# Scores of two dilated heads side by side in two halves of the rows, and a column load moved behind the exponentials of lambda

## The chip, the cores and the metric

The kernel runs on one NeuronCore of a Trainium2 chip. The metric is the device time of one execution in microseconds (us). The engines named here are TensorE (PE in the rows, its weight loads PEld), VectorE (DVE), ScalarE (ACT), GpSimd (POOL) and SyncE (SP), which issues most of the DMAs.

## The reference, cut to what matters

A decoder block on 256 tokens of width 1024: a norm, one projection, attention by 16 heads of 64 columns, an output projection, a norm, and a mixture of 32 experts (top 4). Eight heads are differential (two softmax maps of 32 columns each, subtracted with the scalar lambda, then a norm per head with a weight of 64 numbers, `diff_subln_w`), eight are dilated (one map of 64 columns, a mixture of three patterns of distances):

```python
lam = exp(sum(lq1 * lk1)) - exp(sum(lq2 * lk2)) + lam_init
o_diff = rms_norm(diff_attention(dq, dk, dv, diff_slopes, lam), diff_subln_w) * (1.0 - lam_init)
o_dil = dilated_attention(lq, lk, lv, dil_slopes)
x = x + concatenate([o_diff, o_dil]) @ w_out
x = x + moe_ffn(rms_norm(x, ffn_norm_w), ...)      # 32 experts, 12 MB of f32 weights each
return rms_norm(x, final_norm_w)
```

## The kernel before, in words

Everything is f32 and written out by hand: each engine has a program of its own, in the order in which it is written, and engines wait on counting semaphores.

SP issues all large loads in one queue: x, `w_in` in 13 pieces, the expert biases, then, as the ring slots come free, `w_out` and the expert weights. The ring `gu_ring` has 16 slots of 1 MB, loaded two at a time; `dn_ring` has four. The first experts' loads are written behind waits on counts of TensorE's progress. In the expert loop (`load_gu_half`, line 295 and those after it) each load waits for `gu_used` or `dn_used`, which TensorE raises as it uses a slot up.

TensorE first transposes x, projects (`project`, L567 for the transposed chunks, L572 for the values), and then goes through the 16 heads in a loop over g (line 680). Step g holds, in this order: the three transposes of head g-1's probabilities (`turn_probs`, L545), the scores of head g+1 (`score`, L617 and L618), pieces of other products to fill the time (`FILL`: the rest of the projection, up to g = 8; `OUT`: the output projection, L664, from g = 9), sometimes a transpose of the mixed heads (`turn_mix`, L545 too), and the product of head g-1's probabilities with the values (`pv`, L642 to L644). A head's scores have 256 columns for the second half of the queries and 128 for the first, in one PSUM bank per map. A differential head has two maps, in two groups of 32 rows and in banks 4 and 5. A dilated head has one map in 64 rows, rows 0 to 63 for an even head and 64 to 127 for an odd one, and always in bank 4. Heads 0 to 7 are differential, 8 to 15 dilated.

VectorE's step g is: `negated_scores(g+1)` (L975 takes the scores out of PSUM, L981 finds the extremes), then head g's probabilities (`diff_probs` L988 to L993, `dil_probs` L1006 to L1009); beside that, in some steps, casts of the biases (L945, L950), the scaling of projected chunks (L938), or the norm of two differential heads (`norm_pair`, L1016 to L1023). Probabilities of head g from g = 10 on also wait for head g-2's output copy. ScalarE's step g copies the transposed probabilities of head g-1 (L437), computes the exponentials of head g+1 (L429), copies the transposed mix (L456) and head g-1's output (L442, L447).

The head norm's weight is loaded as a column, twice, into two halves of the partitions of `prm` (two DMAs of 64 elements, L390, third and fourth in ScalarE's queue). VectorE multiplies the column by 1 - lam_init (L967) after it has made lambda's sums and before the loop over heads. ScalarE first uses it in `keep_mixT(0)`, in its step 4. Lambda's exponentials are L410.

After the heads the output projection, the router and the choice of the experts follow, then the loop over 16 pairs of experts: L777 gathers tokens, L822 is gate and up, L837 is down, L796 adds an expert's output to the sums, with four products of 64 rows each, alternately rows 0 to 63 and 64 to 127.

Of the kernel before, what the change touches and what calls it, by code (L numbers as in the profile page):

```python
# [28 lines left out]
P = 128  # L29
T, D = 256, 1024  # L30
TT = T // P
KT = D // P
HD = 64
NH = 8
DK = HD // 2
EPS = 1e-5
LAM_INIT = 0.8 - 0.6
# [12 lines left out]
def moe_block(nc, x, attn_norm_w, w_in, lq1, lk1, lq2, lk2, subln_w, w_out, ffn_norm_w, router_w, router_b,  # L50
              w_gate_up, b_gate_up, w_down, b_down, final_norm_w, out):
    ctx = ExitStack()
    with ctx:
        def sb(name, shape, dt=F32):
            return ctx.enter_context(nc.sbuf_tensor(name, shape, dt))

        def sem(name):
            return ctx.enter_context(nc.semaphore(name))
# [11 lines left out]
        prm = sb("prm", [P, 17])  # L70
# [6 lines left out]
        qkT = gu_ring[:, 13:15, :].rearrange("p s (m t) -> p (s m) t", t=T)  # L77
# [52 lines left out]
        psum = ctx.enter_context(nc.psum_tensor("psum", [P, 8, 512], F32))  # L130
        bank = [psum[:, i, :] for i in range(8)]
# [40 lines left out]
        qk_ready = sem("qk_ready")  # L172
# [3 lines left out]
        scores_done = sem("scores_done")  # L176
        scores_read = sem("scores_read")
# [11 lines left out]
        sub_in = sem("sub_in")  # L189
        sub_ready = sem("sub_ready")  # L190
# [195 lines left out]
        def _(act):  # L386
            act.dma_start(prm_rows[0:8, :], attn_norm_w.rearrange("o (k p) -> (o k) p", p=P)).then_inc(prm_in, 16)
            act.dma_start(prm_rows[8:16, :], ffn_norm_w.rearrange("o (k p) -> (o k) p", p=P)).then_inc(prm_in, 16)
            for i in range(2):
                act.dma_start(prm[HD * i:HD * (i + 1), 16:17], subln_w.rearrange("o d -> d o")).then_inc(sub_in, 16)  # L390

            def squares(a):

# [14 lines left out]
                                         scale=prm[:, k:k + 1]).then_inc(hT_ready_a, 1)  # L408
            act.wait_ge(lam_sum, 1)
            nc.scalar.activation(st[:, 6:8], st[:, 4:6], ACT.Exp).then_inc(lam_exp, 1)  # L410

            def keep_v(done, n, b0, c0):
                act.wait_ge(done, n)
                act.wait_ge(rs_ready, 1)
                for a in range(TT):
                    last = nc.scalar.activation(vS[:, a, c0:c0 + 512], bank[b0 + a][:, :], ACT.Copy,
                                                scale=st[:, 2 + a:3 + a])
                last.then_inc(v_ready, 1)
# [114 lines left out]
            for a in range(TT):  # L533
                act.wait_ge(acc_done, a + 1)
                b = (0, 5)[a]
# [5 lines left out]
        def _(pe):  # L541
            mm = nc.tensor.matmul
# [60 lines left out]
                project(DQK, k)  # L603

            def score(g):
                if g in (0, 4, NH):
                    pe.wait_ge(qk_ready, {0: 2, 4: 4, NH: 8}[g])
                if g >= 1:
                    pe.wait_ge(scores_read, g)
                h = g % NH  # L610
                maps = 2 if g < NH else 1
                rows = HD // maps
                for m in range(maps):
                    r0 = HD * (h % 2) + rows * m
                    tq, tk = (h // 2, 4 + h // 2) if g < NH else (8 + h // 2, 12 + h // 2)
                    q, k = qkT[r0:r0 + rows, tq, :], qkT[r0:r0 + rows, tk, :]
                    mm(bank[4 + m][:, 0:T], q[:, P:T], k, start=True, stop=True)  # L617
                    last = mm(bank[4 + m][:, T:T + P], q[:, 0:P], k[:, 0:P], start=True, stop=True)  # L618
                last.then_inc(scores_done, 1)

            def turn_probs(g):
                pe.wait_ge(probs_ready, g + 1)
                if g == 0:
                    pe.wait_ge(v_ready, 1)
                if g >= 1:
                    pe.wait_ge(probsT_ready, g)
                for b in range(3):
                    last = turn(bank[6][:, P * b:P * (b + 1)], probs[g % 2][:, P * b:P * (b + 1)])
                last.then_inc(probsT_done, 1)
# [16 lines left out]
            def turn_mix(kt, g):  # L646
                if kt < NH // 2:
                    pe.wait_ge(mix_ready, kt + 1)
                pe.wait_ge(pv_read, g - 1)
                if kt >= 1:  # L650
                    pe.wait_ge(mixT_ready, kt)
                for a in range(TT):
                    last = turn(bank[7][:, P + P * a:2 * P + P * a], hmix[:, a, P * kt:P * (kt + 1)])
                last.then_inc(mixT_done, 1)
# [16 lines left out]
            def out_project(kt, a):  # L671
                for c in range(2):
                    out_half(kt, a, c)
# [6 lines left out]
            for g in range(2 * NH):  # L680
                if g == 1:
                    pe.wait_ge(qk_ready, 3)
                    project(EQ, 0)
                    project(EQ, 1)
                if g >= 1:
                    turn_probs(g - 1)
                if g + 1 < 2 * NH:
                    score(g + 1)
                for i, (chunk, k) in enumerate(FILL.get(g, ())):
                    if k == 0:  # L690
                        pe.wait_ge(qk_ready, {EK: 4, EV: 6}[chunk])
                    project(chunk, k)
                    if i == 0 and g in TURN_AT:
                        turn_mix(TURN_AT[g], g)
                if g in TURN_AT and TURN_AT[g] >= NH // 2:
                    turn_mix(TURN_AT[g], g)
                for i, (kt, a) in enumerate(OUT.get(g, ())):
                    out_project(kt, a)
                    if i == 0 and g in TURN_AT and TURN_AT[g] < NH // 2:
                        turn_mix(TURN_AT[g], g)  # L700
                if g >= 1:
                    pv(g - 1)
# [187 lines left out]
        def _(dve):  # L890
            V = nc.vector
# [50 lines left out]
            def rest_of_bias(n):  # L942

                rows = slice(NE * (2 - n), 2 * NE)
                link(V.tensor_tensor(bias_rest[rows, :], (bias_rows if n == 2 else bias_rest)[rows, :], bias3[rows, :],  # L945
                                     ALU.subtract))

            def bias_part(n):
                rows = slice(NE * (2 - n), 2 * NE)
                return V.tensor_copy(bias3[rows, :], bias_rest[rows, :])  # L950
# [7 lines left out]
            for i in range(2):  # L958
                ins = V.tensor_tensor_reduce(out=lam_rows[:, 2 * i, :], in0=lam_rows[:, 2 * i, :],
                                             in1=lam_rows[:, 2 * i + 1, :], scale=1.0, scalar=0.0,  # L960
                                             op0=ALU.mult, op1=ALU.add, accum_out=st[:, 4 + i:5 + i])
# [1 line left out]
                    link(ins)  # L963
            ins.then_inc(lam_sum, 1)

            dve.wait_ge(sub_in, 16 * 2)
            V.tensor_scalar(prm[:, 16:17], prm[:, 16:17], 1.0 - LAM_INIT, None, ALU.mult).then_inc(sub_ready, 1)  # L967
            def negated_scores(g):

                dve.wait_ge(scores_done, g + 1)  # L970
                slope = SLOPES[2 * (g % NH) + (g >= NH)]
                dist = dist_diff if g < NH else dist_dil
                maps = 2 if g < NH else 1
                s = scores[g % 2]
                V.scalar_tensor_tensor(out=s[:, 0:maps, :], in0=dist.unsqueeze(1).broadcast_to([P, maps, T + P]),  # L975
                                       scalar=slope, in1=psum[:, 4:4 + maps, 0:T + P], op0=ALU.mult,
                                       op1=ALU.subtract).then_inc(scores_read, 1)
                dve.wait_ge(scores_read, g + 1)
                for c, w, i in ((0, T, 2), (T, P, 0)):
                    lo = 24 + 4 * (g % 2) + i  # L980
                    ins = V.tensor_reduce(st[:, lo:lo + maps], s[:, 0:maps, c:c + w], AX.X, ALU.min)  # L981
                ins.then_inc(max_ready, 1)
# [53 lines left out]
            for g in range(2 * NH):  # L1036
                if g + 1 < 2 * NH:
                    negated_scores(g + 1)
                if g < NH:
                    diff_probs(g)  # L1040
                else:
                    dil_probs(g)
                if g == 1:
                    rest_of_bias(1)
                if g == 2:
                    bias_part(1).then_inc(bias_split, 1)
                if g == NH - 2:
                    dve.wait_ge(ek_done, 1)
                    for h in range(2):
                        keep_qk(12 + 2 * h, 2 + h, 1.0)  # L1050
                if g >= 3 and g % 2 == 1 and g <= NH + 1:
                    norm_pair((g - 3) // 2)
                if g == 4:
                    dve.wait_ge(eq_used, 4)
                    for h in range(2):
                        keep_qk(8 + 2 * h, h, HD ** -0.5)
# [118 lines left out]
            for r in range(2, ROUNDS):  # L1175
                link(V.scalar_tensor_tensor(out=st[:, 55:56], in0=st[:, 54:55], scalar=float(CAP * r), in1=st[:, 55:56],
                                            op0=ALU.is_gt, op1=ALU.add))
# [53 lines left out]
            for a in range(TT):  # L1231
# [3 lines left out]
                for c in range(2):  # L1235
                    V.scalar_tensor_tensor(out=hmix[:, a, 512 * c:512 * (c + 1)], in0=bank[(0, 5)[a] + c][:, :],
                                           scalar=st[:, 2 + a:3 + a], in1=gu_ring[:, 0, 512 * c:512 * (c + 1)],
                                           op0=ALU.mult, op1=ALU.mult).then_inc(h_ready, 1)
# [21 lines left out]
```

## Time and profile before

| | |
|---|---|
| median of 3 runs (lowest, highest) | 1086.72 us (1086.65, 1087.52) |
| the profiled execution: time, span | 1088.17 us, 1086.4 us |
| mean granted TensorE clock | 0.987 |
| busy in the span: TensorE, VectorE, ScalarE, GpSimd | 1029.8, 228.8, 119.5, 10.1 us |
| moved by DMA | 423.69 MB, mean 390 GB/s |
| issue to landing, medians: `w_in` pieces of 1 MB, of 0.5 MB; x | 18.4, 8.1; 3.7 us |

The rows of the next section come from that one execution. Times run from the first instruction. A matmul of f32 data shows as two records, and the records overlap in time; the distance from one start to the next tells more than a duration. In the chain of waits, which is followed back from the last instruction, a piece's length is what it adds to the chain.

### The profile page before, as it was taken

The page shows a single profiled execution, that of the slowest core. Times are in us where ns is not written, and L with a number is a line of the kernel's source. Part 1 is how long each engine was busy: PE and PEld are TensorE (multiplying, and loading weights), DVE is VectorE, ACT ScalarE, POOL GpSimd, SP SyncE. Part 2 cuts the span into 40 slices and gives each one's busy share as a digit, 9 for nine tenths or more (in the row PEclk, how much of TensorE's full clock was granted, in tenths as well). Part 3 has the DMA queues.
Part 4 walks back from the last instruction along what each step waited for, and adds up shares of the span by engine and source line. Part 5 has one row for each costly group of instructions (what it writes and reads, how often), then busy time and mean ns, then how long its engine had stood idle before and what let it go on. Part 6 is the DMA issues. An engine that isn't in the chain of part 4 may idle for free.

```text
span 1086.4 us, 12314 instructions
## 1 busy us (share of the span) xinstructions
PE 1029.8 (95%) x4971; PEld 442.3 (41%) x4971; DVE 228.8 (21%) x508; ACT 119.5 (11%) x287; POOL 10.1 (1%) x25
## 2 busy tenths in 40 slices
PE   7999999999999999989999999899999999999996
PEld 6686554333343432424242424343243434343422
DVE  3566444111111110111111111111111111111111
ACT  1133430000000000000000000000000000000001
POOL 0000000000000000000000000000000000000000
PEclk9999999999999998999999999999999999999999
DMA  9926546999999999999999999999999999999995
GB/s 283 415 103 243 208 171 264 426 429 427 430 428 428 428 428 430 428 429 428 427 431 427 429 428 428 430 427 428 429 427 431 427 428 430 427 431 427 428 428 207
DMA packets 35808, 423.69 MB, mean 390 GB/s; under 512 B 6016, under 2 KB 6032, under 8 KB 11120
## 3 DMA queue, kind: packets, MB, share of 16 engines
q1 hardware_dynamic: 34032, 423.33, 92.7%
q10 hardware_dynamic: 1760, 0.14, 0.1%
q8 instruction: 10, 0.16, 0.1%
q14 instruction: 6, 0.05, 0.0%
HBM read 422.41 MB, written 1.05 MB: 390 GB/s over the span
## 4 chain that ended last, share of the span: by engine, by line
PE 62%; DMA 31%; DVE 4%; ACT 1%; issue 1%; SPq 0%; DVEq 0%; POOLq 0%; POOL 0%; ACTq 0%
PE psum L822 24%; DMA dn_ring<-in_w_down_dram 23%; PE psum L837 17%; DMA gu_ring<-in_w_gate_up_dram 7%; PE psum L567 5%; PE psum L777 5%; PE psum L545 3%; PE psum L664 3%; PE psum L572 2%; DVE shared L1206 1%; DVE shared L1202 1%; DVE shared L1204 1%; PE psum L617 1%; DMA gu_ring<-in_w_in_dram 1%; ACT shared L519 0%
## 5 line engine op out<-in xcount | busy, mean ns | idle before, releaser
L822 PE MATMUL psum<-gu_ring,shared 128*64 128x512 f32 x2048 | 446.8, 593 | 4.7 <-DMA gu_ring<-in_w_gate_up_dram 4.7
L837 PE MATMUL psum<-dn_ring,shared 128*64 128x512 f32 x1024 | 240.1, 620 | 31.7 <-DMA dn_ring<-in_w_down_dram 30.0
L822 PEld LDWEIGHTS psum<-gu_ring,shared 128*64 128x64 f32 x2048 | 143.5, 137 | 287.4 <-issue 275.1
L837 PEld LDWEIGHTS psum<-dn_ring,shared 128*64 128x64 f32 x1024 | 72.9, 142 | 180.4 <-issue 132.2
L1202 DVE TENSOR_SCALAR shared<-psum 128x512 f32<-128x512 f32 x32 | 22.1, 692 | 398.0 <-PE psum L822 398.0
L1151 DVE TENSOR_TENSOR shared<-posm,iota 128x256 f32<-128x256 f32 x47 | 20.0, 425 | 291.1 <-PE psum L545 290.6
L517 ACT ACTIVATE shared<-psum 128x512 f32<-128x512 f32 x32 | 19.1, 597 | 436.7 <-PE psum L822 436.7
L796 PE MATMUL psum<-shared 64*128 64x512 f32 x264 | 65.6, 615 | 0.7 <-ACT shared L510 0.7
L777 PE MATMUL psum<-shared,xres 128*128 128x128 f32 x512 | 63.0, 282 | 1.0 <-DVE shared L1121 1.0
L777 PEld LDWEIGHTS psum<-shared,xres 128*128 128x128 f32 x512 | 61.7, 197 | 1.5 <-DVE shared L1121 1.5
L567 PE MATMUL psum<-gu_ring 128*128 128x256 f32 x256 | 59.3, 390 | 2.1 <-DMA gu_ring<-in_w_in_dram 2.1
L510 ACT ACTIVATE shared<-psum 128x512 f32<-128x512 f32 x32 | 19.1, 597 | 317.5 <-PE psum L837 317.5
L567 PEld LDWEIGHTS psum<-gu_ring 128*128 128x128 f32 x256 | 49.3, 195 | 10.1 <-issue 2.9
L545 PE MATMUL psum<-ident,shared 128*128 128x128 f32 (+1 forms) x243 | 46.8, 300 | 3.0 <-ACT shared L519 0.7
L545 PEld LDWEIGHTS psum<-ident,shared 128*128 128x128 f32 (+1 forms) x243 | 30.6, 180 | 38.7 <-issue 25.7
L796 PEld LDWEIGHTS psum<-shared 64*128 64x128 f32 x264 | 22.8, 186 | 43.0 <-issue 41.4
L1164 DVE TENSOR_TENSOR shared<-psum,ffn_p 128x512 f32<-128x512 f32 x32 | 22.1, 692 | 59.9 <-PE psum L777 59.9
L801 PE MATMUL psum<-shared 96*64 96x512 bf16 x192 | 32.9, 395 | 0.0
L664 PE MATMUL psum<-dn_ring,shared 128*128 128x512 f32 x64 | 30.1, 602 | 0.0
L572 PE MATMUL psum<-gu_ring 128*128 128x512 f32 x64 | 29.3, 601 | 0.0
L519 ACT ACTIVATE shared<-psum 128x512 f32<-128x512 f32 x32 | 19.1, 597 | 80.2 <-PE psum L545 80.2
L429 ACT ACTIVATE shared<-shared,st 128x256 f32<-128x256 f32 (+1 forms) x48 | 20.6, 445 | 40.1 <-DVE st L981 40.1
(142 smaller groups left out, 354.0 us busy)
## 6 DMA issues: line engine op xcount, KB each, us to landing
gu_ring<-in_w_gate_up_dram SPq DMA_DIRECT2D x128, 2048.0 KB, 26.4
dn_ring<-in_w_down_dram SPq DMA_DIRECT2D x64, 2048.0 KB, 23.4
gu_ring<-in_w_in_dram SPq DMA_DIRECT2D x11, 1024.0 KB, 18.4
dn_ring<-in_w_out_dram SPq DMA_DIRECT2D x4, 1024.0 KB, 8.9
xres<-in_x_dram SPq DMA_DIRECT2D x2, 512.0 KB, 3.7
gu_ring<-in_w_in_dram SPq DMA_DIRECT2D x2, 512.0 KB, 8.1
out_dram<-hmix SPq DMA_DIRECT2D x4, 256.0 KB, 2.0
dn_ring<-in_b_gate_up_dram SPq DMA_DIRECT2D x3, 256.0 KB, 15.1
```

Source lines behind the costliest of these rows:

```text
L429: last = nc.scalar.activation(s[:, m, c:c + w], s[:, m, c:c + w], ACT.Exp, bias=st[:, lo + i + m:lo + i + m + 1], scale=-1.0, **acc)
L545: return nc.tensor.transpose(dst, src, ident[0:rows, 0:rows])
L567: last = mm(bank[b][:, c:c + T], w[:, P * (m0 + m):P * (m0 + m + 1)], hT[:, k, :], start=(k == 0 and m % 2 == 0), stop=(k == KT - 1), skip ...
L572: last = mm(bank[b0 + a][:, :], hT[:, k, P * a:P * (a + 1)], w[:, v0:v0 + 512], start=(k == 0), stop=(k == KT - 1))
L664: last = mm(bank[2 * a + c][:, :], mixT[:, kt, P * a:P * (a + 1)], dn_ring[:, kt // 2, w0:w0 + 512], start=(kt == 0), stop=(kt == KT - 1))
L777: last = mm(bank[b][:, c:c + P], rows, sel[:, a, :, :].rearrange("p e n -> p (e n)"), start=(a == 0), stop=(a == TT - 1))
L796: last = mm(bank[(0, 5)[a] + c][:, :], combT[rows, P * a:P * (a + 1)], yrow[rows, :], start=False, stop=True, skip_group_check=True)
L801: return mm(bank[b][CAP * c:CAP * (c + 1), :], bias_sel[half][0:3 * NE, :], bias3[0:3 * NE, col:col + 512], start=True, stop=False, skip_g ...
L822: last = mm(bank[2 + b][CAP * c:CAP * (c + 1), :], xg[:, k, CAP * half:CAP * (half + 1)], gu_ring[:, 8 * half + k, w0:w0 + 512], start=Fal ...
L837: last = mm(bank[4][CAP * c:CAP * (c + 1), :], actT[:, a0:a0 + CAP], dn_ring[:, k // 2, w0:w0 + 512], start=False, stop=(k == KT - 1), ski ...
L1164: V.tensor_tensor(xg[:, 4 * b:4 * b + 4, :], bank[XG_BANKS[first][b]][:, :].rearrange("p (k n) -> p k n", k=4), ffn_p[:, 4 * b:4 * b + 4]. ...
L1202: chain(V.tensor_scalar(up_t, bank[3][:, :], 1.0 - LIMIT, 1.0 + LIMIT, ALU.max, ALU.min))
```

## The change

The first edit takes the dilated heads out of `score` and adds `score_pair`, which is called in steps 7, 9, 11 and 13 and computes the scores of two dilated heads: the even one from rows 0 to 63 into bank 4, the odd one from rows 64 to 127 into bank 5, the products alternating between them. Each head raises `scores_done` by one as before. The even steps from 8 to 14 compute no scores. VectorE reads bank 4 or 5 by the head. The second edit moves the two column loads in ScalarE's queue behind the exponentials of lambda, and VectorE's wait for them with the multiplication into its step 2, behind the last cast of the biases.

```diff
 # ScalarE
             act.dma_start(prm_rows[8:16, :], ffn_norm_w.rearrange("o (k p) -> (o k) p", p=P)).then_inc(prm_in, 16)
-            for i in range(2):
-                act.dma_start(prm[HD * i:HD * (i + 1), 16:17], subln_w.rearrange("o d -> d o")).then_inc(sub_in, 16)
...
             nc.scalar.activation(st[:, 6:8], st[:, 4:6], ACT.Exp).then_inc(lam_exp, 1)
+            for i in range(2):
+                act.dma_start(prm[HD * i:HD * (i + 1), 16:17], subln_w.rearrange("o d -> d o")).then_inc(sub_in, 16)
 # TensorE
             def score(g):
-                if g in (0, 4, NH):
-                    pe.wait_ge(qk_ready, {0: 2, 4: 4, NH: 8}[g])
+                if g in (0, 4):
+                    pe.wait_ge(qk_ready, {0: 2, 4: 4}[g])
                 if g >= 1:
                     pe.wait_ge(scores_read, g)
                 h = g % NH
-                maps = 2 if g < NH else 1
-                rows = HD // maps
-                for m in range(maps):
-                    r0 = HD * (h % 2) + rows * m
-                    tq, tk = (h // 2, 4 + h // 2) if g < NH else (8 + h // 2, 12 + h // 2)
-                    q, k = qkT[r0:r0 + rows, tq, :], qkT[r0:r0 + rows, tk, :]
+                for m in range(2):
+                    r0 = HD * (h % 2) + DK * m
+                    q, k = qkT[r0:r0 + DK, h // 2, :], qkT[r0:r0 + DK, 4 + h // 2, :]
                     mm(bank[4 + m][:, 0:T], q[:, P:T], k, start=True, stop=True)
                     last = mm(bank[4 + m][:, T:T + P], q[:, 0:P], k[:, 0:P], start=True, stop=True)
                 last.then_inc(scores_done, 1)
+
+            def score_pair(g):
+
+                if g == NH:
+                    pe.wait_ge(qk_ready, 8)
+                pe.wait_ge(scores_read, g)
+                heads = [(qkT[HD * m:HD * (m + 1), 4 + g // 2, :], qkT[HD * m:HD * (m + 1), 8 + g // 2, :]) for m in range(2)]
+                for m, (q, k) in enumerate(heads):
+                    mm(bank[4 + m][:, 0:T], q[:, P:T], k, start=True, stop=True)
+                for m, (q, k) in enumerate(heads):
+                    mm(bank[4 + m][:, T:T + P], q[:, 0:P], k[:, 0:P], start=True, stop=True).then_inc(scores_done, 1)
...
                     turn_probs(g - 1)
-                if g + 1 < 2 * NH:
+                if g + 1 < NH:
                     score(g + 1)
+                elif g % 2 and g + 1 < 2 * NH:
+                    score_pair(g + 1)
 # VectorE
-            dve.wait_ge(sub_in, 16 * 2)
-            V.tensor_scalar(prm[:, 16:17], prm[:, 16:17], 1.0 - LAM_INIT, None, ALU.mult).then_inc(sub_ready, 1)
             def negated_scores(g):
...
-                maps = 2 if g < NH else 1
+                maps, b = (2, 4) if g < NH else (1, 4 + g % 2)
                 s = scores[g % 2]
                 V.scalar_tensor_tensor(out=s[:, 0:maps, :], in0=dist.unsqueeze(1).broadcast_to([P, maps, T + P]),
-                                       scalar=slope, in1=psum[:, 4:4 + maps, 0:T + P], op0=ALU.mult,
+                                       scalar=slope, in1=psum[:, b:b + maps, 0:T + P], op0=ALU.mult,
                                        op1=ALU.subtract).then_inc(scores_read, 1)
...
                 if g == 2:
                     bias_part(1).then_inc(bias_split, 1)
+                    dve.wait_ge(sub_in, 16 * 2)
+                    V.tensor_scalar(prm[:, 16:17], prm[:, 16:17], 1.0 - LAM_INIT, None, ALU.mult).then_inc(sub_ready, 1)
```

## Rows read from the trace of the kernel before

**Rows 1.** The page, part 2: DMA share and rate in 40 slices.

```profile
DMA  9926546999999999999999999999999999999995
GB/s 283 415 103 243 208 171 264 426 429 427 430 428 428 428 428 430 428 429 428 427 431 427 429 428 428 430 427 428 429 427 431 427 428 430 427 431 427 428 428 207
```

**Rows 2.** Windows: stretch, busy time and records of each engine, clock, DMA share, GB/s.

```profile
118.00:124.00 6.00, 5.45 (x23) 3.07 (x21) 3.32 (x13) 2.41 (x7) 1.01 (x1) 1.00 1.01 426
170.00:176.00 6.00, 6.00 (x35) 3.05 (x36) 2.87 (x9) 1.49 (x2) 0.00 (x0) 1.00 0.00 0
```

**Rows 3.** Timeline of SP from 170 us: start, length, DMA issues.

```profile
175.62 10.54 SPq L263 DMA_DIRECT2D gu_ring<-in_w_gate_up_dram  x4
```

**Rows 4.** Chain that ended last, in order of time: start, length, what.

```profile
18.83 13.82 PE psum L567 x64
...
79.45 0.64 PE psum L617 x4
80.09 0.22 PE psum L618 x4
...
100.54 0.63 PE psum L617 x2
101.17 0.22 PE psum L618 x2
...
123.49 0.48 ACT shared L456
...
171.76 13.88 PE psum L822 x64
```

**Rows 5.** Timeline of TensorE at heads 12 and 13: start, length, operation, shapes.

```profile
125.22 0.70 PE L617 MATMUL psum<-gu_ring 64*128 64x256 f32 x2
...
128.68 0.50 PE L545 MATMUL psum<-ident,shared 128*128 128x128 f32 x3
...
132.39 0.49 PE L545 MATMUL psum<-ident,shared 128*128 128x128 f32 x3
```

**Rows 6.** The same chain: products of 512 columns, on 128 and on 64 rows.

```profile
40.00 3.43 PE psum L572 x8
...
187.56 1.92 PE psum L796 x8
```

**Rows 7.** Timeline of VectorE, 115 to 130 us.

```profile
120.11 0.43 DVE L1023 TENSOR_TENSOR hmix<-hmix,st 128x256 f32<-128x256 f32 x1 [1.12 <-POOL st L365]
121.36 0.56 DVE L975 SCALAR_TENSOR_TENSOR shared<-shared,psum 128x384 f32<-128x384 f32 x1 [0.83 <-PE psum L618]
...
126.18 0.55 DVE L975 SCALAR_TENSOR_TENSOR shared<-shared,psum 128x384 f32<-128x384 f32 x1 [2.74 <-PE psum L618]
...
128.09 0.17 DVE L1009 RECIPROCAL st<-st 128x2 f32<-128x2 f32 x1
```

**Rows 8.** Timeline of ScalarE at the first and the 12th head's exponentials.

```profile
46.38 0.51 ACT L429 ACTIVATE shared<-shared,st 128x256 f32<-128x256 f32 x1 [12.03 <-DVE st L981]
...
122.60 0.80 ACT L429 ACTIVATE shared<-shared,st 128x256 f32<-128x256 f32 x2 [1.52 <-DVE st L981]
```

**Rows 9.** Instructions on prm: min/median/max ns, first and last start; its loads' landing.

```profile
L407 ACT ACTIVATE gu_ring<-psum,prm x4: 466/470/474, 7.4 to 19.0; 128x256 f32<-128x256 f32 x4
...
L390 ACTq DMA_DIRECT2D prm<-in_diff_subln_w_dram x2: 526/567/608, 1.8 to 2.3; - x2
...
DMA to landing us min/median/max: 7.0/7.2/7.4
```

**Rows 10.** Timeline of VectorE, 73 to 77 us.

```profile
73.45 0.95 DVE L975 SCALAR_TENSOR_TENSOR shared<-shared,psum 128x768 f32<-128x768 f32 x1
...
76.94 0.35 DVE L993 SCALAR_TENSOR_TENSOR shared<-shared,st 128x128 f32<-128x128 f32 x1
```

**Rows 11.** TensorE's first projection in the timeline, and a window before it.

```profile
9.43 8.96 PE L567 MATMUL psum<-gu_ring 128*128 128x256 f32 x32 [2.08 <-DMA gu_ring<-in_w_in_dram]
6.00:7.00 1.00, 1.00 (x6) 0.89 (x5) 0.93 (x3) 0.00 (x0) 0.00 (x0) 1.00 0.49 131
```

## The prediction

> **What bounds the kernel now.** I read the page first for stages. Its slices [rows 1] show two: up to about slice 6 (some 170 us) the DMA share moves between 0.2 and 0.9; from slice 7 on the DMA share stands at 9 and the rate at 426 to 431 GB/s to the end. A window says it closer for the last of the first stage [rows 2]: no byte moves from 170 to 176 us, and then the stream is full. So the expert loop is paced by the weight stream, and what counts is when the stream starts. It starts at 175.62 us, where SP issues the load into the first ring slot that TensorE has used up [rows 3]; TensorE's first use of that slot begins at 171.76 us [rows 4]. Nothing else that the stream needs is late then, since the queues had been empty for some six us. So a microsecond that TensorE saves before 171.76 us moves the stream, and with it the end, by that microsecond; a microsecond saved on TensorE in the loop is worth nothing.
>
> Then the chain of waits through the stretch that the change touches, 100 to 172 us [rows 4]. It is TensorE nearly throughout: the two score rows of a head (0.63 and 0.22 us), then the next products with no gap. The other engines take it over in three places between 99 and 141 us only. The largest waits are for the transposed mix that ScalarE copies, the second of these at 123.49 us [rows 4]; the other kind is for a head's output before the next transpose of the mix.
>
> **The change part by part.**
>
> *Removed: the scores of heads 9, 11, 13 and 15 as steps of their own.* A dilated head's scores hold the chain for 0.63 + 0.22 = 0.85 us [rows 4] (at 100.54 and 101.17). Two records are one f32 product. A product of 512 columns takes 3.43 / 4 = 0.86 us [rows 6], so 384 columns take 0.64 us; the other 0.21 us of the 0.85 are spent around it, where TensorE goes from 128 rows to 64 and back. All eight dilated heads repeat the pattern. Four of the eight go: 4 x 0.85 = 3.40 us.
>
> *Added: two more products in each of the four pairs that stay.* What a pair costs, the trace of before shows twice. A differential head has two maps in two groups of 32 rows and two banks, 768 columns in four products. They hold the chain for 0.64 + 0.22 = 0.86 us [rows 4] (at 79.45 and 80.09), what a dilated head's two products take; one after another they would take 1.28 + 0.21 = 1.49 us. And for halves of 64 rows: the combine of the experts puts four products of 512 columns alternately on the two halves, 8 records in 1.92 us, against 3.43 us for the same columns on all 128 rows [rows 6]; 1.92 - 0.21 = 1.71 is two products, not four. So halves do run beside each other at 64 rows too. I take 0.85 us for a pair, as for one head now, thus nothing added. The bounds: 0.85 and 1.49 us, so 0 to 4 x 0.64 = 2.56 us added in all. The pair also signals twice where a head signals once; no row here isolates the second signal. By the Trainium skill, page "TensorE: Matmul & The Clock Gate", section "The cost: per-tile semaphore tail", increments serialize at some 26 ns each; by that, an estimate, the four pairs would lose 0.1 us, and the sum would be 3.3 and not 3.4.
>
> *New order: does something else become late?* In the loop over heads, an even step now has no scores, an odd one has those of the next two heads. In an odd step VectorE works on the first of the pair as now: scores start at 125.22, VectorE starts at 126.18, ends head 11's probabilities at 128.09 + 0.17 = 128.26, TensorE wants them at 128.68 [rows 5, 7]: 0.42 us to spare, unchanged as long as the pair's first head is as fast as a single one. In an even step TensorE arrives 0.85 us sooner: for head 12's at 132.39 - 0.85 = 131.54 us. VectorE had waited for TensorE there, but need not now, since head 13's scores lie ready: it goes on at 128.26 and needs another 126.18 to 128.26 = 2.08 us, so 130.34: over one us to spare. ScalarE is tightest at head 11: its scores have to wait for the head norm, which ends on VectorE at 120.11 + 0.43 = 120.54; ScalarE starts the exponentials 1.24 us after VectorE starts on the scores (121.36 to 122.60) and takes 0.80, so until 122.6, just when the transposed mix, 0.85 us earlier than 123.49, wants its copy [rows 4, 7, 8]. Say 0 to 0.1 us lost there. The three waits above stay: each follows a transpose or an output, not scores. For new waits I take 0.1 us, and as the bound what would undo all four even steps' savings but one, 2.5 us.
>
> *Moved: the two column loads of the norm weight.* At the head of ScalarE's queue they took 0.53 and 0.61 us to issue and landed after 7.0 and 7.4 us [rows 9]. In the new place, behind the exponentials of lambda (which end 12.03 us before 46.38, at 34.35), ScalarE has nothing until 46.38 [rows 8]: the 1.2 us of issue are hidden. VectorE now wants them where it starts head 4's scores, at 73.45 us [rows 10]. Issued by 35.5 us they may take 38 us to land; the loads of 1 MB that queue through the same full stretch take 18.4 at the median (the table above). So the wait costs nothing. The multiplication of one column (0.17 us at most, what its row on two columns takes, at 128.09 in [rows 7]) now stands in its queue in front of head 4's scores. Behind it, head 3's probabilities are ready at 76.94 + 0.35 = 77.29 and wanted by the transposes that precede 79.45, 0.50 us long as those at 128.68, thus at 78.95 [rows 4, 5, 10]. So the 0.17 us are hidden 1.66 us deep.
>
> What goes from the start is the load pair itself. TensorE's first projection waits 2.08 us for its weights and starts at 9.43 us; the DMA share falls to 0.49 in the microsecond from 6 to 7 [rows 11], and the columns, issued at 1.8 and 2.3 us, land at about 9.3, just after. If the columns cause it, up to 9.43 - 7.87 = 1.56 us is to be had: at 7.4 + 0.47 = 7.87 us the first transposed tile is there, the next thing that the projection waits for [rows 9] (the row of L407). If they don't, nothing. Their own bytes are 0.5 KB. Later in this kernel a larger set of small pieces (the router's weight and the second norm weight, issued by ScalarE behind head 7) is in flight while the rate is 426 GB/s, from 118 to 124 us [rows 2], so I take zero. By the Trainium skill, page "DMA: Bandwidth & Descriptors", section "Rules for kernel authors", a load whose last dimension is not contiguous becomes one descriptor per element, 128 here, whereas its section "Issuing engines are not separate DMA queues" has such loads merely interleave with the others; the first speaks for the 1.56 us, the second for zero.
>
> *Sum:* 3.40 - 0 - 0.1 = 3.3 us. The profiled execution took 1088.17 us, 1.8 around its span of 1086.4; it would take 1084.9. It stands 1.45 above the median of the runs; the saving is the same there: 1086.7 - 3.3 = 1083.4 us.
>
> **Rivals.**
> 1. *The start moves too.* The dip around 6 us goes with the columns: 3.3 + 1.5 = 4.8, thus 1081.9 us. For it: the columns land just as the first weights do, and the dip has no other owner that I can name. Against: 0.5 KB, and the row from 118 us on. The first 32 records of the projection take 8.96 us [rows 11], 280 ns each, against 216 ns later (13.82 us for 64 [rows 4]); an earlier start could shorten that too, by up to 2.0 us, and add to it.
> 2. *New waits eat it.* Heads in twos make TensorE wait for VectorE or ScalarE in the even steps; half is lost: 1.6 us gained, 1085.1 us. For it: 0.42 us to spare is little. Against: the sums above.
> 3. *The halves do not overlap.* Pairs of 1.49 us: 3.40 - 2.56 = 0.84 gained, 1085.9 us; only the four changes of row shape are saved. Against: both patterns of [rows 4, 6].
> 4. *Slower: the columns come late.* VectorE's queue stands at 73.45 us until both have landed, before head 4's scores. TensorE has 1.66 us to spare (77.29 to 78.95), the gain buys 3.3 more; so from a landing at 78.4 us on, 43 us after the issue, the kernel is slower, and at 50 us after it by 7 us: 1094. Against: 18.4 us for 1 MB in that stretch, and 7.4 for the columns before.
>
> **How the numbers follow.** Chances: the forecast 0.62, start moves too 0.16, waits eat it 0.11, no overlap 0.06, late columns 0.03, something unnamed of either sign 0.02. The likeliest gives 1083.4. The range, 1081.3 to 1085.2, takes in the first rival with half a us beyond it and most of the second; beyond lie the third, the fourth and the tails. No change from 0.2% (2.17 us, about what a measurement of this kernel tells from no change) leaves: faster 0.62 + 0.16 + 0.01 = 0.79, same 0.11 + 0.06 = 0.17, slower 0.03 + 0.01 = 0.04.
>
> **What would show it.** In the profile after: pairs of 0.85 us at four places, the last of them near 133, and none in even steps; the three waits of TensorE still there and no fourth; the first expert product at 168.4 and SP's issue at 172.2 instead of 171.76 and 175.62, with the stream full from there; first projection still at 9.4 us. A pair row of 1.3 us or more says rival 3, a wait for VectorE at a transpose of probabilities in an even step rival 2, a first projection before 9 us rival 1. If TensorE's gain up to 171.76 us is there but the end has not moved with it, my reading of the stream is wrong.

## The result and the profile after

The changed kernel takes 1082.45 us at the median of five runs (1080.44 to 1083.12), the kernel before, on the same chip, 1087.52 (1086.65 to 1089.01). The ratio is 0.9949 with a 95% interval of 0.9938 to 0.9960, a gain of 5.1 us (4.3 to 6.7) where 3.3 were forecast and 1083.4 us as the time. The profiled execution was the fastest of the five: 1080.44 us with a span of 1078.7, 7.7 us under the span of before. That this one is a special case came out only in the experiments. (One run of e9 below, at 1117.5 us with a lower granted clock, is left out of its median and range.)

The page of the changed kernel, part 2, DMA share and rate in 40 slices. It answers to [rows 1]: the stream fills from slice 7 on as before, at the same rate.

```profile
DMA  9935467999999999999999999999999999999995
GB/s 326 383 140 241 171 234 299 426 427 428 430 429 429 428 428 428 429 428 428 428 428 428 430 429 428 428 428 428 430 428 428 428 428 428 428 430 430 427 427 211
```

SP's timeline (it answers to [rows 3]) and the chain of waits (to [rows 4, 6]) of the changed kernel. In its lines L614 and L615 are the differential scores, L625 and L627 the pairs, L650 to L652 the products with the values, L832 is gate and up.

```profile
168.21 10.54 SPq L263 DMA_DIRECT2D gu_ring<-in_w_gate_up_dram  x4
```

```profile
7.92 7.17 PE psum L567 x32
...
36.70 3.43 PE psum L572 x8
...
97.25 0.63 PE psum L625 x4
97.88 0.22 PE psum L627 x4
98.11 5.35 PE psum L572 x12
...
104.07 0.34 PE psum L545 x3
104.40 1.72 PE psum L572 x4
...
118.15 0.46 ACT shared L456
...
164.35 13.88 PE psum L832 x64
```

Three things are to be seen. A pair (768 columns) holds the chain for 0.63 + 0.22 us, as one head's 384 columns did. An even step has no scores: the transposes at 104.07 are followed by the next product at once. And that product's four records take 1.72 us. In the chain of before the same step read:

```profile
107.35 0.34 PE psum L545 x3
107.68 0.63 PE psum L617 x2
108.31 0.22 PE psum L618 x2
108.53 1.91 PE psum L572 x4
```

So 0.63 + 0.22 + 0.19 = 1.04 us went with the step, not 0.85: its scores, and what the four records behind them had taken more, 1.91 - 1.72. From the first value product (40.00 before, 36.70 now) to the first expert product (171.76, 164.35) it is 131.76 us before and 127.65 now: 4.11 us. The remaining 3.30 us of this profile lie ahead of 36.70. SP's first issue of the loop moved by 175.62 - 168.21 = 7.41 us, the span by 7.7: what is gained ahead of the stream arrives at the end.

### The profile page after: what moved, and what is told of

The parts are those of the page before. It is cut to its first block, busy times and chain, and to the rows that moved or that the text cites. A ratio compares the mean times of both kernels' runs of the same rounds, so it can differ in the third digit from the quotient of the medians.

```text
span 1078.7 us, 12314 instructions
## 1 busy us (share of the span) xinstructions
PE 1025.4 (95%) x4971; PEld 438.7 (41%) x4971; DVE 228.5 (21%) x508; ACT 119.2 (11%) x287; POOL 10.1 (1%) x25
## 4 chain that ended last, share of the span: by engine, by line
PE 64%; DMA 28%; DVE 5%; ACT 1%; issue 1%; SPq 0%; POOL 0%; DVEq 0%; POOLq 0%; ACTq 0%
PE psum L832 25%; DMA dn_ring<-in_w_down_dram 21%; PE psum L847 18%; DMA gu_ring<-in_w_gate_up_dram 7%; PE psum L787 6%; PE psum L567 5%; PE psum L545 3%; PE psum L572 2%; PE psum L672 2%; DVE shared L1216 1%; DVE shared L1212 1%; DVE shared L1214 1%; PE psum L614 0%; ACT shared L519 0%; PE psum L652 0%
## 5 line engine op out<-in xcount | busy, mean ns | idle before, releaser
L832 PE MATMUL psum<-gu_ring,shared 128*64 128x512 f32 x2048 | 446.8, 593 | 4.8 <-DMA gu_ring<-in_w_gate_up_dram 4.8
L832 PEld LDWEIGHTS psum<-gu_ring,shared 128*64 128x64 f32 x2048 | 143.5, 137 | 287.5 <-issue 274.7
L572 PE MATMUL psum<-gu_ring 128*128 128x512 f32 x64 | 29.2, 599 | 0.0
## 6 DMA issues: line engine op xcount, KB each, us to landing
dn_ring<-in_b_gate_up_dram SPq DMA_DIRECT2D x3, 256.0 KB, 14.1
```

The source lines that it names most:

```text
L572: last = mm(bank[b0 + a][:, :], hT[:, k, P * a:P * (a + 1)], w[:, v0:v0 + 512], start=(k == 0), stop=(k == KT - 1))
L832: last = mm(bank[2 + b][CAP * c:CAP * (c + 1), :], xg[:, k, CAP * half:CAP * (half + 1)], gu_ring[:, 8 * half + k, w0:w0 + 512], start=Fal ...
```

## The experiments

Two questions: how the 7.4 us divide, and why the runs as a whole gained only five. Theory: each half of the change adds its part, 3.3 us for the columns and 4.1 for the pairs. Rival: the early start of the one profile is chance.

**e1, the columns alone**, scores one head at a time:

```diff
             act.dma_start(prm_rows[8:16, :], ffn_norm_w...)
-            for i in range(2):
-                act.dma_start(prm[HD * i:HD * (i + 1), 16:17], subln_w.rearrange("o d -> d o")).then_inc(sub_in, 16)
...
             nc.scalar.activation(st[:, 6:8], st[:, 4:6], ACT.Exp).then_inc(lam_exp, 1)
+            for i in range(2):
+                act.dma_start(prm[HD * i:HD * (i + 1), 16:17], subln_w.rearrange("o d -> d o")).then_inc(sub_in, 16)
```

(and VectorE's wait and multiplication as in the change)

> Only the column loads are moved, the scores stay one head at a time. Theory (each half of the change adds its own part: the two column loads at the head of ScalarE's queue delay TensorE's first projection weights by 1.5 us and its faster pace by another 1.8): first projection at 7.9 us, in the step loop everything 3.3 us earlier than before, first expert product at 171.8 - 3.3 = 168.5 us, span 1083, time 3.3 us under before. Rival (the early start of the one profiled execution is chance, and the columns have no part in it): first projection anywhere from 7.9 to 9.4 us whatever stands in the queue, time within 1 us of before.

**e2, the pairs alone**, columns at the head of the queue as before (the second edit undone):

```diff
             act.dma_start(prm_rows[8:16, :], ffn_norm_w...)
+            for i in range(2):
+                act.dma_start(prm[HD * i:HD * (i + 1), 16:17], subln_w.rearrange("o d -> d o")).then_inc(sub_in, 16)
...
```

(gone behind the exponentials of lambda, and VectorE's wait and multiplication back in their old place)

> Only the scores are paired, the column loads stay at the head of ScalarE's queue. Theory: each even step from 8 to 14 is 1.04 us shorter (0.85 for the scores and 0.19 for the next product, which follows a change of row shape), so 4.1 us in all, first projection at 9.4 us, first expert product at 171.8 - 4.1 = 167.6 us, time 4.1 us under before. Rival (start is chance): the same steps, but the first projection may stand at 7.9 us, and the time is that of the full change.

**e3, the changed kernel once more**, no edit:

> The changed kernel once more, for a second profile and for times on the same chip as the two halves. Theory: first projection at 7.9 us again, first expert product at 164.3, time 3.3 + 4.1 = 7.4 us under before in an execution whose loop is undisturbed; the two halves add up. Rival (start is chance): first projection at some other time in this profile, and the time equals that of the pairs alone, 4.1 to 5 us under before.

**e4, rows in the place of the columns:**

```diff
             act.dma_start(prm_rows[8:16, :], ffn_norm_w...)
+            for i in range(2):
+                act.dma_start(scratch[i:i + 1, :], subln_w).then_inc(scratch_in, 16)
...
```

(`scratch` is a new tile that nothing reads, and the program waits at its end until both loads have landed)

> The changed kernel with two more loads in the place where the column loads stood, third and fourth in ScalarE's queue: the same 64 numbers, but as a contiguous row of 256 bytes into one partition each (a scratch that nothing reads). Theory A (the shape of the column loads, 64 pieces of 4 bytes each, holds up the weights): no delay, first projection at 7.9 us, time as the changed kernel. Theory B (any two further loads on ScalarE's queue in that moment do it): first projection at 9.4 us, time 3.3 us above the changed kernel.

All four ran on one chip beside the kernel before (1087.27 us, 17 runs, 1085.01 to 1089.15):

| kernel | median us (range) | ratio to before (95%) | first projection | its first 32 records | first value product | from there to the first expert product |
|---|---|---|---|---|---|---|
| before (first profile) | 1087.27 (1085.01 to 1089.15) | | 9.43 | 8.96 | 40.00 | 131.76 |
| e1 columns alone | 1086.89 (1084.68 to 1087.97) | 0.9995 (0.9986 to 1.0003) | 8.27 | 10.04 | 39.92 | 131.77 |
| e2 pairs alone | 1082.68 (1081.43 to 1083.66) | 0.9954 (0.9941 to 0.9968) | 8.29 | 9.26 | 39.16 | 127.63 |
| e3 both | 1083.00 (1081.77 to 1083.65) | 0.9956 (0.9944 to 0.9969) | 7.93 | 9.81 | 39.34 | 127.63 |
| e4 both, rows at the head | 1082.63 (1082.12 to 1083.03) | 0.9955 (0.9943 to 0.9967) | 7.92 | 9.49 | 39.02 | 127.63 |

The pairs are all of the gain that can be measured: 4.1 us from value product to expert product in each profile with them, and 4.6 us in the times of e2, to which moving the columns adds nothing that shows (e3 is 0.3 us above e2, both intervals nearly alike). My theory of two parts failed on the columns: e1 gained 0.4 us, and its interval reaches from a loss of 0.3 to a gain of 1.5, so 3.3 us are excluded and half a microsecond is not. The rival, chance, is right for the 3.3 us of the first profile. But it is not right on the DMAs. The windows from 6 to 8 us (columns as in [rows 2]), first of e2 with columns at the head:

```profile
6.00:7.00 1.00, 1.00 (x5) 0.65 (x4) 0.93 (x3) 0.00 (x0) 0.00 (x0) 1.00 0.63 172
7.00:8.00 1.00, 0.64 (x4) 0.24 (x2) 0.58 (x3) 0.60 (x2) 0.00 (x0) 1.00 0.67 193
```

then of e3 without them:

```profile
6.00:7.00 1.00, 1.00 (x6) 0.75 (x5) 0.93 (x3) 0.00 (x0) 0.00 (x0) 1.00 1.03 414
7.00:8.00 1.00, 0.61 (x4) 0.21 (x2) 0.68 (x3) 0.60 (x2) 0.00 (x0) 1.00 1.03 410
```

and of e4 with rows in their place:

```profile
6.00:7.00 1.00, 1.00 (x6) 0.72 (x5) 0.93 (x3) 0.00 (x0) 0.00 (x0) 1.00 1.00 406
7.00:8.00 1.00, 0.65 (x4) 0.25 (x2) 0.65 (x3) 0.61 (x2) 0.00 (x0) 1.00 1.06 406
```

So the dip of [rows 11] is the columns' doing, by their shape (64 pieces of 4 bytes, each to a partition of its own) and not by the number of loads or their bytes: 512 bytes cost the stream over half of its rate for some us. The dip is there in both profiles with the columns at the head and in none without. The packets of ScalarE's queue in the first 12 us tell the shapes apart, here before, in the changed kernel and in e4:

```profile
q10 hardware_dynamic: 192, 0.01, 0.9%
...
q10 hardware_dynamic: 32, 0.01, 0.3%
...
q10 hardware_dynamic: 36, 0.01, 0.3%
```

With the two columns the queue has 160 packets more, with the two rows four. Whether the number of pieces or that of the partitions they go to does the harm, e4 does not separate.

Where did the earlier start go? Into the pace of the first projection. In e1 it starts 0.35 us later than in the first profile of the changed kernel (7.92 and 7.17, above) and takes 2.87 us longer:

```profile
8.27 10.04 PE psum L567 x32
```

The starts of the single records show why: they follow each other at first after 427 ns and later after 216, at half pace and then at full pace, the two levels of TensorE's clock (1.2 and 2.4 GHz). The distance changes at 13.12 us before, at 14.14 in e1, 12.58 in e2, 13.29 in e3, 12.65 in e4 (12.20 and 13.42 in e7 and e8 below), but at 7.85 us, ahead of the projection, in the changed kernel's first profile. The windows' clock column stands at 1.00 all through and does not show it: each trace's record of the clock begins only at the time just named, with the full clock, and has nothing for the stretch ahead of it. While the pace is half, a microsecond of earlier start is worth half a microsecond of work. In e1 the start is 1.16 us earlier than before, worth 0.58, and the full pace comes 1.02 us later, which costs 0.51: the first value product stands 0.08 us earlier, at 39.92. This made the next theory: what ends the slow pace is TensorE's work, not the time since the start, and it can be had early.

**e5, idle products** in the two empty stretches of the start:

```diff
+            def idle_products(n):
+                for _ in range(n):
+                    mm(bank[3][:, 0:P], ident[:, :], ident[:, :], start=True, stop=True)
+
+            idle_products(7)
             pe.wait_ge(x_in[0], 16)
...
             for k in range(4):
                 turn_x(1, k)
+            idle_products(3)
             for k in range(KT):
```

> The changed kernel with products of the identity with itself, whose results nothing reads, in TensorE's two empty stretches of the start: seven before x has landed, three before the first projection. Theory (after the column move TensorE starts its projection up to 1.5 us earlier, but its records keep the slow pace of 430 ns until 13 or 14 us whenever it starts, and so give the start back; what ends the slow pace is how long TensorE has been at work without a gap): records at 216 ns from before 9 us, first 32 records of the projection in 7.0 to 7.5 us as in the one lucky profile, first expert product at 164.3 to 164.8 us, time 2 to 3 us under the changed kernel. Rival (the end of the slow pace is set by something outside TensorE, such as the time since the start): slow until 13 us as before, time unchanged or up to 0.5 us longer for the added products.

**e6, the same with the columns at the head**, as in e2:

> As the warmed kernel, but with the column loads at the head of ScalarE's queue, where they stood before the change. Theory (the columns' own price is the late first weights, 0.4 to 1.5 us, and it is hidden in the plain kernel only because the slow pace ends at the same time anyway): now the late start counts in full, first projection at 8.3 to 9.4 us, time 0.4 to 1.5 us over the warmed kernel with moved columns. Rival (the columns never cost anything): first projection and time equal to the warmed kernel's within 0.3 us.

**e9, idle products in the kernel before**, nothing else:

> The kernel before with the idle products in TensorE's two empty stretches of the start, and nothing else. Theory (the pairs save 4.13 us whatever the start does; the spread of the kernel before, 1085 to 1089 us, comes from where the slow pace ends): values sum within 1 us, first 32 records of the projection in 7.0 to 7.3 us, first expert product at 37.3 + 131.8 = 169.1 us, time 4.1 us over the warmed kernel with pairs and the columns at the head (1081.0), thus 1085.1. Rival (the idle products help the paired kernel only, or something in the loop spreads the times): spread as without them, time 1087.

| kernel | median us (range) | first projection | its first 32 records | first value product | to the first expert product |
|---|---|---|---|---|---|
| e5 changed, idle products | 1080.54 (1080.20 to 1080.68) | 8.36 | 7.07 | 37.04 | 127.64 |
| e6 the same, columns at the head | 1081.03 (1080.47 to 1082.15) | 8.55 | 7.14 | 37.30 | 127.64 |
| e9 before, idle products | 1085.1 (1084.54 to 1086.23) | 9.35 | 7.14 | 38.10 | 131.77 |

The timeline of TensorE in e5: the first row are the idle products, the transposes at 4.74 still run at the slow pace, the projection does not.

```profile
1.59 3.36 PE L583 MATMUL psum<-ident 128*128 128x128 f32 x14 [1.59 <-POOL ident L349]
4.74 1.91 PE L545 MATMUL psum<-ident,xres 128*128 128x128 f32 x8
...
7.69 0.83 PE L583 MATMUL psum<-ident 128*128 128x128 f32 x6
8.36 7.07 PE L567 MATMUL psum<-gu_ring 128*128 128x256 f32 x32
```

The theory holds: in the five kernels with idle products the full pace comes at 5.45 to 7.67 us, always ahead of the projection. e5 is 2.5 us under e3 (1083.00 to 1080.54, two chips' medians of before being 0.4 apart, in the other direction), and the times of its six runs lie within 0.5 us where e3's spread over 1.9 and the kernel before's, on e5's chip, over 4.2. e9 gains 2.8 us on the kernel before of its chip (1087.94), so the idle products do not help the paired kernel only, and its time is the expected one. Its values spread over 1.7 us, not within the 1 us expected; before they spread over 3.4 there. So about half of that kernel's spread goes with the slow pace. e9 also gives the pairs once more, on a quieter ground: 1085.1 - 1081.03 = 4.1 us between e9 and e6 (two chips, their medians of before 0.3 apart), and 4.13 in the profiles.

And e6 gives the columns a price. The wait for the first weights is back (0.62 us idle, projection 0.2 to 1.0 us later in e6 and e9 than in e5), the median is 0.5 us higher than e5's, though both intervals against before overlap, and the range is 1.7 and not 0.5:

```profile
8.55 7.14 PE L567 MATMUL psum<-gu_ring 128*128 128x256 f32 x32 [0.62 <-DMA gu_ring<-in_w_in_dram]
```

All profiles together bear it out: the projection starts at 8.29 to 9.43 us in the five with the columns at the head and at 7.92 to 8.36 in the eight without. And of the kernels with idle products those with the columns at the head spread over 1.7 us (e6, e9), those without over 0.4 to 0.5 (e5 and, below, e10 and e11). The profile of e9:

```profile
9.35 7.14 PE L567 MATMUL psum<-gu_ring 128*128 128x256 f32 x32 [1.80 <-DMA gu_ring<-in_w_in_dram]
```

**e8, the price of the change of row shape.** The kernel before with the dilated scores over all 128 rows:

```diff
                 for m in range(maps):
...
+                    if g >= NH:
+                        r0, rows = 0, P
                     q, k = qkT[r0:r0 + rows, tq, :], qkT[r0:r0 + rows, tk, :]
```

> The kernel before, but each dilated head's scores taken over all 128 rows instead of its own 64, so that two heads' scores are summed (the output is not the reference's): the same columns and banks, no change of row shape. Theory (1.04 us per score step are 0.64 for 384 columns and 0.40 for the change to 64 rows and back, half of it showing in the product that follows): a score step takes 0.64 us up to the next product and four following records 1.72 and not 1.91 us; eight heads are 3.2 us shorter. Rival (64-row products are slower in themselves): the same 0.2 us around the scores stays, only 0 to 0.2 us saved per head.

Measured once: 1085.01 us. Its chain:

```profile
106.84 0.33 PE psum L545 x3
107.18 0.43 PE psum L619 x2
107.61 0.22 PE psum L620 x2
107.83 1.72 PE psum L572 x4
```

0.65 us for the scores and 1.72 for the next four records, 0.39 less than with 64 rows; where a transpose of the mix follows the scores it is 0.3 to 0.35. From the first value product (39.88) to the first expert product (168.77) it is 128.89, 2.87 less than before where 3.2 were expected. Hence 1.04 = 0.65 + 0.39. The rival, that 64-row products are slower in themselves, e8 alone does not exclude, since it takes away the narrow products together with the change. The starts of the single records do. Before, at this place, the four score records start at 107.61, 107.93, 108.15 and 108.26, in e8 at 107.01, 107.23, 107.45 and 107.56: the second distance and the third are the same, and only the first is 0.10 us longer, as is the one from the transpose to the scores (0.20 and not 0.11). Behind the scores it is the same again, 0.20 and 0.53 us into the product of 128 rows and not 0.11 and 0.43. So the 0.39 us go with the change, and 64-row products that follow each other are not slower.

**e7, filling work dealt out anew**, against the two waits for the transposed mix that the change left alone:

```diff
-                6: [(EV, 0), (EV, 1)], 7: [(EV, 2), (EV, 3), (EV, 4)], ...
+                6: [(EV, 0), (EV, 1), (EV, 2)], 7: [(EV, 3), (EV, 4)], ...
-        OUT = {9: [(0, 1), (0, 0)], 10: [(1, 0)], ...
+        OUT = {9: [(0, 1)], 10: [(0, 0), (1, 0)], ...
```

> The changed kernel with the filling work dealt out differently: one more projection piece in step 6 and one fewer in step 7, and the product of the first output chunk with the second token tile's queries moved from step 9 to step 10, behind the transposed mix. Theory (the two waits of 0.61 and 0.66 us for ScalarE's copy of the transposed mix are uncovered because nothing stands between the transpose and the product that waits): both waits gone, first expert product 1.2 us earlier relative to the start of the heads, time 1.2 us less. Rival (the waits come back as waits for probabilities in steps 7 and 10, which now come sooner): less than 0.4 us gained.

1081.51 us (1079.52 to 1081.89), 1.5 under e3's median on another chip; in the profile 126.70 us from value to expert product, 0.95 less where 1.2 were expected. The first wait is gone, of the second 0.24 us remain:

```profile
119.97 0.41 PE L650 MATMUL psum<-gu_ring,shared 128*128 128x64 f32 x2 [0.24 <-ACT shared L456]
```

The chain of e7 says why the rest stays: it runs from 112.94 to 119.84 us over VectorE, GpSimd and ScalarE (head 11's scores and the norm of two heads, then the exponentials and the copy), so from 112.94 on TensorE's order of work no longer shortens it.

**e10, both; e11, both with six and one idle products** instead of seven and three:

> The changed kernel with idle products and with the other dealing of the filling work together. Theory (both parts lie on the path to the first expert product and do not touch each other): 1080.5 - 0.95 = 1079.6 us, first expert product at 163.7. Rival (one swallows the other's gain): 1080.5.

> As the one with both, but six idle products ahead of x and one ahead of the first projection, instead of seven and three. Theory (seven and three overshoot: x's transposes started at 4.74 where x is there at 4.35, the projection at 8.36 where its operands are there at 7.92): projection at 7.95 to 8.1 us with the full pace, 0.3 us less, 1079.3 us. Rival (the shorter busy stretch leaves the pace slow into the projection): first 32 records in 8 us and more, time 1080 to 1082 with a wide spread.

e10 takes 1079.57 us (1079.51 to 1079.92), e11 1079.59 (1079.50 to 1079.95), each at a ratio to before of 0.9923 (0.9910 to 0.9936): 8.4 us under the kernel before (1087.94 there), the best of the study. The parts add up. The smaller number of idle products gains nothing, where 0.3 us were expected: e11's projection starts at 7.92 instead of 8.03 us and takes 7.17 instead of 7.08, and the first value product stands at 36.70 and 36.71.

## Why the prediction was right, and where its terms were off

- **What bounds:** right. All that was gained before the first expert product came out at the end: 7.41 us in SP's issue against 7.7 in the span, with the loop's stream at 428 GB/s in both.
- **Scores removed, 3.40 us:** the mechanism right, the term too small. It measured 4.11 to 4.14 us (six profiles with pairs against three without), 1.03 per step. The 0.85 us were read to the start of the next product; the chain of before had the rest in plain sight, four records of L572 in 1.91 us behind scores and in 1.72 elsewhere. e8 and the single records show what it is: the first product in the other row shape pays too.
- **Pairs cost nothing more:** right, 0.63 + 0.22 us for 768 columns. The second signal per pair shows in no row. The 0.1 us, an estimate for four pairs from the 26 ns per increment of the Trainium skill (page "TensorE: Matmul & The Clock Gate", section "The cost: per-tile semaphore tail"), are not to be seen here. The halves of 64 rows run beside each other as the combine's had.
- **New waits, 0.1 us:** none. Head 11's exponentials did become the last thing ahead of the copy of the transposed mix, as reckoned (the row at 118.15 in the chain), and TensorE's wait there is 0.66 us as before. But nothing is to spare there any more: from 111.63 to 118.62 us the chain runs over VectorE, GpSimd and ScalarE, where before it ran over TensorE until 123.49. In even steps VectorE ended head 12's probabilities with 0.85 us to spare (126.00 less 125.15) where over one was forecast, since TensorE came 1.04 us sooner and not 0.85, and it waited 0.19 us for ScalarE's output copy:

```profile
124.18 0.42 DVE L1014 SCALAR_TENSOR_TENSOR shared<-shared 128x256 f32<-128x256 f32 x1 [0.19 <-ACT hmix L447]
...
124.98 0.17 DVE L1017 RECIPROCAL st<-st 128x2 f32<-128x2 f32 x1
```

- **Columns moved, nothing at the new place:** right. Landed 5.3 to 5.6 us after an issue at 30.3, wanted at 70.15; the multiplication took 0.15 us and delayed nobody (instructions on prm, changed kernel; [rows 9] before):

```profile
L410 ACTq DMA_DIRECT2D prm<-in_diff_subln_w_dram x2: 535/570/606, 30.3 to 30.8; - x2
...
L1056 DVE TENSOR_SCALAR prm<-prm x1: 154/154/154, 70.2 to 70.2; 128x1 f32<-128x1 f32 x1
...
DMA to landing us min/median/max: 5.3/5.4/5.6
```

- **Columns gone from the start, taken as nothing:** right in the time (e1: 0.4 us, interval -0.3 to 1.5), by a reason that I did not have. I took zero because I doubted that 512 bytes could hold up a stream. They do: the two arguments against the first rival, the bytes and the undisturbed rate from 118 us on [rows 2], were no arguments, as the windows of e2 and e4 show. On the dip, the rule on strided loads of the Trainium skill, page "DMA: Bandwidth & Descriptors", section "Rules for kernel authors", was the better guide than its section on how DMAs of several engines interleave; the queue's 160 packets more are of the order of its 128 descriptors. What keeps the gain small is the slow pace, which I had seen (280 ns a record against 216) and had down only as something that might add: it halves what an earlier start is worth, and in e1 it also lasted longer.
- **The rival "the start moves too", 1081.9 us:** the first profile looks just like it, 7.7 us, and e3, the same kernel, shows that it is one execution in several. Had I judged by that profile alone I would have given the columns 3.3 us that they don't earn. The rivals on overlap, on new waits and on late columns fell. The sign that I named for the early start, a first projection before 9 us, was no sign: e2 and e8 have the columns at the head and start at 8.29 and 8.89. Nor could the last pair be near 133 us, which is its place before: by the sum it is 132.88 - 3 x 0.85 = 130.3, and e3 has it at 129.13.

The measured gain at the median, 5.1 us in the first five runs and 4.3 in e3, is 4.13 us of pairs. The rest, 0.2 to 0.9 us, is no more than what a slow pace that ends sooner or later makes of the first value product in the profiles, but the runs without a profile do not show theirs, so this part is argued. That 1083.4 us came so near to 1082.45 and to e3's 1083.00 is in part luck: the pairs gave 0.8 us more than the sum had, and the base of 1086.72 lay 0.8 us under the 1087.52 of the five runs.

## What to carry to other kernels

Price an instruction group by what the chain loses without it, up to the point where the following work is back at its usual length: a change of the array's row shape is paid half by the product behind it. A part at the start of a kernel that falls in TensorE's slow stretch should be judged by several profiles or by the end of that stretch, since a start made earlier is worth only half while it lasts; products on data that is there anyway cost nothing in empty time and took 2.5 us away here, and most of the spread once the columns were moved too. Two products in different halves of the rows and in different banks are had for the price of one.

## What the runs showed of the hardware that was not expected

- Two loads of 64 single elements each, in flight beside large ones, held the 16 engines at 0.42 to 0.79 of their time from 6 to 9 us (e2, e6, e8, e9, the kernel before), while two contiguous loads of the same bytes did not (1.00 and over in e4).
- TensorE ran its records at half pace until 12.2 to 14.1 us in seven profiles, though it was at work from 4.1 to 4.4 us on with one gap of 0.4 to 2.1 us ahead of the projection, and until 7.85 us in one that looks no different (its gap was 0.25 us). With products from 1.59 us on, the full pace came between 5.4 and 7.7 us in each of five. What decides between 8 and 12 to 14 us without them stays open.
- Going from 128 rows to 64 and back costs 0.39 to 0.40 us, 0.20 at the scores and 0.19 in the product behind; in between, records on 64 rows follow each other as fast as on 128.
